# Where the root and the reciprocal of the last RMS norm are taken: one transformer-like block on one core of a Trainium2 chip

## The chip, the cores and the metric

The kernel runs on one core of one Trainium2 chip. The core has a matrix engine (PE, TensorE; its weight loads are shown as PEld), VectorE (DVE), ScalarE (ACT), GpSimd (POOL) and SyncE (SP, which here only issues DMAs), and 16 DMA engines. The metric is the device time of one execution in microseconds (us), median of several runs. All times below are in us unless marked ns.

## What is computed

One block on 512 tokens of width 1024 in fp32: a norm, a mixer of three branches (banded attention, gated spatial mixing, a linear recurrence), a second norm, a mixture of 16 experts of which each token takes two, and a last norm over the sum. The change touches the last norm only:

```
def rms_norm(x, g):
    x32 = x.astype(jnp.float32)
    y = x32 * lax.rsqrt(jnp.mean(x32 * x32, axis=-1, keepdims=True) + EPS)
    return (y * g.astype(jnp.float32)).astype(x.dtype)
...
        x = x + hierarchical_moe(xn, router_grp_w[l], router_grp_b[l], router_exp_w[l], router_exp_b[l],
                                 exp_w_gate[l], exp_w_up[l], exp_w_down[l])
    return rms_norm(x, final_norm_g)
```

## The kernel before

There is no scheduler: each engine's program is written out by hand, in one function for each engine, and semaphores order the engines against each other. From about 480 us to 760 us the experts run. A loop over tiles of 128 token slots takes 16 blocks of expert weights per tile. A block of 128 x 1024 fp32 (512 KB) is loaded by SP into one of two sets of buffers, in pieces of 512 columns (2,048 bytes) for each partition; only the last expert's up-projection comes in pieces of 256 columns (1,024 bytes). The buffers lie in the tiles `raw`, `raw_a`, `raw_c`, `raw_mg`, `macc` and `xn2T`. ACT copies each block, rounded, to `w_hi` (L378), DVE takes the remainder `w_lo` (L389), and PE multiplies with both (L1048 to L1050). `w_hi` and `w_lo` have four slots each, so that ACT waits until PE has released the slot of four blocks ago; SP reuses a buffer when DVE has made its `w_lo`.

Tiles in SBUF are laid out in the order in which they are declared, each at a multiple of 32 bytes in every partition. In the built program `par`, `raw`, `w_hi`, `w_lo`, `ident`, `tile_table` and `stat` come first, then `minus_half` at byte 75,008, `slot_idx`, `att`, and an unused tile named `to_512`. The tiles declared behind it (`probs_third`, `macc`, `x_rows`, `raw_a`, `raw_mg`, `xn2T`, `gf_rows`, `raw_c` and the rest) begin with `probs_third` at byte 75,264, which is 147 x 512. All the large ones among them begin at a multiple of 512 bytes. `xrT`, too, begins at one; DVE reads it 4, 8 and 12 bytes further in at L1624.

At the end, the 512 tokens are handled as NT = 4 tiles t = 0 to 3 of 128 rows and 1024 columns. POOL gathers for each tile the rows of its two experts from HBM (`gather`, L667) into `y_lo(t)` and `y_hi(t)`, both in `raw_mg` but for the last `y_hi`, which is in `raw`. DVE adds the first expert to the residual (`first_sum`, L2060). PE puts the second one and the slots of the last expert tile together in PSUM, and DVE adds them (`last_sum`, L2073); tile 3 takes its second expert by a DVE instruction instead (`second_sum`, L2067). ACT copies the last expert tile's product out of PSUM in two halves before that (`xT_hi`, L1033), and DVE takes the remainders (L2079).

The norm of a tile has then these steps. ACT squares the rows and accumulates the sum in `stat[:, 6, t]` (L1040). DVE multiplies it by 1/1024 and adds EPS (`last_mean`, L2085). POOL raises it to the power -1/2 into `stat[:, 7, t]` (L683). DVE multiplies the rows by that and by the gains `gf_rows` (`last_norm`, L2090), for tile 3 in two halves, and SP stores them (L575, L579). These steps of the four tiles are interleaved in the order of the code at the end of DVE's function.

## Time and profile before

| | |
|---|---|
| median of 3 runs | 780.43 us (780.24 to 780.47) |
| the profiled execution | 782.81 us, of which the span of the trace 780.8 us |
| PE, DVE, ACT, POOL busy | 763.4, 495.2, 449.9, 208.2 us |
| mean granted PE clock in the span | 0.995 of 2.4 GHz |
| moved by DMA | 206.75 MB, 265 GB/s over the span |

The profile is of one execution, recorded by the chip's profiler, which takes a little longer than the others. The span runs from the first instruction to the last. In the timeline a row has its start, its duration, the engine, the line of the kernel, and the operands with their sizes; `x2` or `x3` are like instructions merged into one row. Instructions of one engine overlap a little, so that what one costs its engine is the distance between starts and not its duration.

### The profile page before, as it was taken

The numbers are of one execution on the slowest core, as the hardware profiler recorded it, in microseconds if no ns is written. First come the engines' busy times: TensorE is split into PE (matmuls) and PEld (weight loads), VectorE is DVE, ScalarE is ACT, GpSimd is POOL, SyncE is SP. The second block draws the span as 40 slices with busy tenths as digits, with TensorE's granted clock in tenths as the row PEclk, the third lists the DMA queues.
The fourth block names the chain that finished last, engine by engine and source line by source line (L and its number), as shares of the span: only waits on it lengthen the run. The fifth ranks groups of instructions, "written<-read, shape, count | busy, mean of one in ns | idle before, by whom it ended". The sixth has DMA issues, their size and how long they took to land.

```text
span 780.8 us, 10780 instructions
## 1 busy us (share of the span) xinstructions
PE 763.4 (98%) x3739; PEld 622.4 (80%) x3739; DVE 495.2 (63%) x698; ACT 449.9 (58%) x590; POOL 208.2 (27%) x124
## 2 busy tenths in 40 slices
PE   7999999999999999999999999999999999999994
PEld 4888777777787888888888888888888888888782
DVE  4374476585853302322022468999999998999888
ACT  6244657565653322323222446888888878888862
POOL 3474433232332444344445222000000000000033
PEclk9999999999999999999999999999999999999998
DMA  8489999792222263323336738999999999999965
GB/s 298 136 275 381 371 343 387 263 352 80 57 79 81 82 205 91 109 82 107 92 98 191 272 125 279 407 409 408 409 409 409 409 409 410 408 409 409 401 242 206
DMA packets 134319, 206.75 MB, mean 265 GB/s; under 512 B 10813, under 2 KB 65669, under 8 KB 134278
## 3 DMA queue, kind: packets, MB, share of 16 engines
q1 hardware_dynamic: 129780, 189.94, 66.8%
q0 software_dynamic: 2304, 8.39, 2.9%
q10 hardware_dynamic: 2194, 7.89, 2.5%
q8 instruction: 24, 0.39, 0.2%
q14 instruction: 17, 0.14, 0.0%
HBM read 157.95 MB, written 48.25 MB: 264 GB/s over the span
## 4 chain that ended last, share of the span: by engine, by line
PE 93%; DMA 2%; POOL 1%; DVE 1%; issue 1%; ACT 1%; ACTq 0%; DVEq 0%; SPq 0%; POOLq 0%
PE ps L1048 28%; PE ps L1050 27%; PE ps L1049 27%; PE ps L1336 2%; PE ps L1140 1%; PE ps L1168 1%; PE ps L1151 1%; PE ps L1289 1%; POOL raw_mg L667 1%; PE ps L1263 1%; DMA x<-in_x 1%; PE ps L1343 1%; DMA raw_mg<-slots,slot_idx 1%; PE ps L1065 1%; PE ps L1193 1%
## 5 line engine op out<-in xcount | busy, mean ns | idle before, releaser
L383 POOL TENSOR_TENSOR w_lo<-raw,w_hi 128x1024 fp32r<-128x1024 f32 x72 | 173.2, 2407 | 245.1 <-ACT w_hi L371 245.1
L371 ACT ACTIVATE w_hi<-raw 128x1024 fp32r<-128x1024 f32 x73 | 76.9, 1058 | 183.5 <-PE ps L1050 170.6
L1048 PE MATMUL ps<-xn_hi,w_hi 128*128 128x512 f32 x352 | 140.6, 399 | 0.0
L1050 PE MATMUL ps<-xn_hi,w_lo 128*128 128x512 f32 x352 | 137.2, 390 | 0.0
L1049 PE MATMUL ps<-xn_lo,w_hi 128*128 128x512 f32 x352 | 137.1, 390 | 0.0
L1048 PE MATMUL ps<-w_hi,xT_hi 128*128 128x512 f32 (+1 forms) x248 | 96.7, 390 | 0.0
L1050 PE MATMUL ps<-w_hi,xT_lo 128*128 128x512 f32 (+1 forms) x248 | 95.1, 384 | 0.0
L1049 PE MATMUL ps<-w_lo,xT_hi 128*128 128x512 f32 (+1 forms) x248 | 94.9, 383 | 0.0
L667 POOL DMA_INDIRECT raw_mg<-slots,slot_idx x7 | 7.8, 1113 | 277.4 <-DMA slots<-y_tile 275.6
L1048 PEld LDWEIGHTS ps<-xn_hi,w_hi 128*128 128x128 f32 x352 | 66.1, 188 | 16.2 <-issue 2.5
L1049 PEld LDWEIGHTS ps<-xn_lo,w_hi 128*128 128x128 f32 x352 | 66.1, 188 | 14.1 <-issue 1.0
L1050 PEld LDWEIGHTS ps<-xn_hi,w_lo 128*128 128x128 f32 x352 | 66.1, 188 | 14.0
L1706 DVE SCALAR_TENSOR_TENSOR macc<-raw,ps 128x512 f32<-128x512 f32 x16 | 11.0, 687 | 94.1 <-PE ps L1050 93.8
L389 DVE TENSOR_TENSOR w_lo<-raw_mg,w_hi 128x1024 fp32r<-128x1024 f32 x57 | 67.6, 1219 | 0.6 <-ACT w_hi L378 0.5
L378 ACT ACTIVATE w_hi<-raw_mg 128x1024 fp32r<-128x1024 f32 x57 | 59.0, 1055 | 6.7 <-PE ps L1050 6.5
L389 DVE TENSOR_TENSOR w_lo<-raw,w_hi 128x1024 fp32r<-128x1024 f32 x43 | 51.6, 1219 | 5.0 <-ACT w_hi L378 4.7
L1048 PEld LDWEIGHTS ps<-w_hi,xT_hi 128*128 128x128 f32 x248 | 46.6, 188 | 9.4 <-DVE w_lo L389 0.7
L1050 PEld LDWEIGHTS ps<-w_hi,xT_lo 128*128 128x128 f32 x248 | 46.6, 188 | 9.3
L1049 PEld LDWEIGHTS ps<-w_lo,xT_hi 128*128 128x128 f32 x248 | 46.7, 188 | 8.5
L378 ACT ACTIVATE w_hi<-raw 128x1024 fp32r<-128x1024 f32 x43 | 44.8, 1056 | 14.0 <-PE ps L1050 10.7
L1048 PE MATMUL ps<-w_hi,hT_hi 128*128 128x512 f32 x128 | 51.3, 401 | 0.6 <-DVE hT_lo L1961 0.6
L1050 PE MATMUL ps<-w_hi,hT_lo 128*128 128x512 f32 x128 | 50.0, 390 | 0.0
(311 smaller groups left out, 1477.6 us busy)
## 6 DMA issues: line engine op xcount, KB each, us to landing
slots<-raw SPq DMA_DIRECT2D x65, 512.0 KB, 7.0
raw<-in_w_in SPq DMA_DIRECT2D x52, 512.0 KB, 4.3
raw_mg<-in_exp_w_down SPq DMA_DIRECT2D x35, 512.0 KB, 11.0
raw<-in_exp_w_gate SPq DMA_DIRECT2D x29, 512.0 KB, 11.8
raw_a<-in_exp_w_gate SPq DMA_DIRECT2D x26, 512.0 KB, 10.9
raw_c<-in_exp_w_up SPq DMA_DIRECT2D x24, 512.0 KB, 11.8
raw_mg<-in_exp_w_up SPq DMA_DIRECT2D x22, 512.0 KB, 10.6
raw<-in_exp_w_up SPq DMA_DIRECT2D x15, 512.0 KB, 11.6
```

The lines of the kernel that those rows point to most:

```text
L371: nc.scalar.activation(w_hi[:, b % HI_SLOTS, :], raw_buf(b), ACT.Copy)\
L378: nc.scalar.activation(w_hi[:, (8 + r) % HI_SLOTS, :], buf, ACT.Copy).then_inc(S["hi_act"], 1)
L383: eng.tensor_tensor(w_lo[:, b % HI_SLOTS, :], raw_buf(b), w_hi[:, b % HI_SLOTS, :].bitcast(F32), ALU.subtract)\
L389: nc.vector.tensor_tensor(w_lo[:, (8 + r) % HI_SLOTS, :], place(at, r)[0], w_hi[:, (8 + r) % HI_SLOTS, :].bitcast(F32), ALU.subtract)\
L667: pool.indirect_dma_start(dst, None, slots, bass.IndirectOffsetOnAxis(ap=slot_idx[:, 2 * t + k:2 * t + k + 1], axis=0))\
L1048: pe.matmul(dst, hi_l, hi_r, start=start, stop=False)
L1049: pe.matmul(dst, hi_l, lo_r, start=False, stop=False)
L1050: return pe.matmul(dst, lo_l, hi_r, start=False, stop=stop)
L1065: mm = pe.transpose(ps[:, 2 * t + k // 4, (k % 4) * P:(k % 4 + 1) * P], x0[:, t, k * P:(k + 1) * P], ident[:, :])
L1140: mm = pe.matmul(score_home(g, h)[:, home + k0:home + k1], qT[rows, jp % 2, i * P:(i + 1) * P], kT[rows, jp % 2, k0:k1], start=True, stop= ...
L1336: mm = pe.transpose(ps[:, 3 + k // 4, (k % 4) * P:(k % 4 + 1) * P], rows[:, k * P:(k + 1) * P], ident[:, :])
L1706: dve.scalar_tensor_tensor(out=macc[:, 1, :], in0=gate_buf[:, g % 3, :], scalar=1.0, in1=ps[:, 2 + c, :], op0=ALU.add, op1=ALU.mult)\
```

## The change

ACT takes the root right behind its square of each tile, `sqrt(sum/1024 + EPS)`, with the scale as a constant and EPS from a new tile `eps_col`, and DVE takes the reciprocal of it in place (`last_rstd`), at which `last_norm` multiplies as before. DVE's `last_mean` and POOL's power are gone. DVE waits for ACT (`y_rms`) before its reciprocal, and for its own reciprocal (`y_rstd`) before `last_norm`. ACT waits for its own square (`y_sq`) before the root. Ahead of the last copies, ACT takes the root of `eps_col` once into an unused place, which puts the loading of the root's table there. POOL sets `eps_col` at the start of the kernel.

```diff
--- before.py
+++ after.py
@@ -144,6 +144,7 @@
 
         stat = sb(ctx, "stat", [P, 8, NT])
         minus_half = sb(ctx, "minus_half", [P, 1])
+        eps_col = sb(ctx, "eps_col", [P, 1])
         slot_idx = sb(ctx, "slot_idx", [P, 2 * NT], I32)
         att = sb(ctx, "att", [P, 3, 4])
         sb(ctx, "to_512", [P, 32])
@@ -293,7 +294,7 @@
             "exp_in exp_done scattered tab "
             "x_even_in x_odd_in xT_ps xT_hi_done xT_done silu_done hid_done hT_ps hT_hi_done hT_done "
             "y_act y_even_stored y_odd_stored y_last_stored before_last_stored sel_ps sel_done z_ps "
-            "y_sum y_sq y_stat y_rstd y_norm y_out dve_chain").split()}
+            "y_sum y_sq y_rms y_rstd y_norm y_out dve_chain").split()}
         raw_in = [sem(f"raw_in{s}") for s in range(RAW_MIX)]
         even_in = [sem(f"even_in{s}") for s in range(PER_TILE)]
         odd_in = [sem(f"odd_in{s}") for s in range(PER_TILE)]
@@ -584,6 +585,7 @@
         def _(pool):
 
             pool.memset(ident[:, :], 0.0).then_inc(S["ident_done"], 1)
+            pool.memset(eps_col[:, :], EPS)
             pool.memset(minus_half[:, :], -0.5).then_inc(S["consts_pool"], 1)
             pool.wait_ge(S["ident_done"], 1)
             pool.affine_select(out=ident[:, :], in_=ident[:, :], compare_op=ALU.not_equal, fill=1.0, base=0,
@@ -678,10 +680,6 @@
             for t in range(NT):
                 gather(0, y_lo(t), t)
                 gather(1, y_hi(t), t)
-            for t in range(NT):
-                pool.wait_ge(S["y_stat"], t + 1)
-                pool.tensor_tensor(stat[:, 7, t:t + 1], stat[:, 6, t:t + 1], minus_half[:, :], ALU.pow)\
-                    .then_inc(S["y_rstd"], 1)
 
 
         @block.scalar
@@ -1028,6 +1026,7 @@
                 if s == 10:
                     hT_hi_half(0)
             hT_hi_half(1)
+            act.activation(att[:, 0, 0:1], eps_col[:, :], ACT.Sqrt)
             for c in range(2):
                 act.wait_ge(S["w_used"], loop_block(tiles, 3 + c))
                 act.activation(xT_hi[:, 4 * c:4 * c + 4, :].rearrange("p k n -> p (k n)"), ps[:, 5 + c, :], ACT.Copy)\
@@ -1039,6 +1038,9 @@
                     act.wait_ge(S["y_sq"], t)
                 act.activation(xn2[:, 0, :], y_lo(t), ACT.Square, accum_out=stat[:, 6, t:t + 1])\
                    .then_inc(S["y_sq"], 1)
+                act.wait_ge(S["y_sq"], t + 1)
+                act.activation(stat[:, 7, t:t + 1], stat[:, 6, t:t + 1], ACT.Sqrt, scale=1.0 / D, bias=eps_col[:, :])\
+                   .then_inc(S["y_rms"], 1)
 
 
         @block.tensor
@@ -2080,10 +2082,9 @@
                                   xT_hi[:, 4 * c:4 * c + 4, :].rearrange("p k n -> p (k n)").bitcast(F32),
                                   ALU.subtract).then_inc(S["xT_done"], 1)
 
-            def last_mean(t):
-                dve.wait_ge(S["y_sq"], t + 1)
-                dve.tensor_scalar(stat[:, 6, t:t + 1], stat[:, 6, t:t + 1], 1.0 / D, EPS, ALU.mult, ALU.add)\
-                   .then_inc(S["y_stat"], 1)
+            def last_rstd(t):
+                dve.wait_ge(S["y_rms"], t + 1)
+                dve.reciprocal(stat[:, 7, t:t + 1], stat[:, 7, t:t + 1]).then_inc(S["y_rstd"], 1)
 
             def last_norm(t, at=slice(0, D)):
                 dve.wait_ge(S["y_rstd"], t + 1)
@@ -2100,16 +2101,16 @@
             last_sum(0)
             first_sum(3)
             last_sum(1)
-            last_mean(0)
             second_sum(3)
             last_sum(2)
-            last_mean(1)
+            last_rstd(0)
             last_norm(0)
             last_sum(3)
-            last_mean(2)
+            last_rstd(1)
             last_norm(1)
-            last_mean(3)
+            last_rstd(2)
             last_norm(2)
+            last_rstd(3)
             for c in range(2):
                 last_norm(3, slice(512 * c, 512 * (c + 1)))
```

`eps_col` takes 32 bytes in each partition, between `minus_half` and `slot_idx`. In the built program every tile declared behind it lies 32 bytes further: `probs_third` begins at byte 75,296, and the large tiles behind it begin 32 bytes past a multiple of 512. `raw`, `w_hi`, `w_lo` and `ident` stay where they were.

ACT's program behind the last copy of `hT_hi`, to its end, before (`xn,stat<-raw_mg` is the square with its sum):

```order
L1007 ACTIVATE hT_hi<-ps 128x256
L1032 ISA
L1033 ACTIVATE xT_hi<-ps 128x512
L1032 REGISTER_ALU
L1033 ACTIVATE xT_hi<-ps 128x512
L1040 ACTIVATE xn,stat<-raw_mg 128x1024 x4
```

The same place now:

```order
L1005 ACTIVATE hT_hi<-ps 128x256
L1029 ACT_TABLE_LOAD
L1029 ACTIVATE att<-eps_col 128x1
L1031 ISA
L1032 ACTIVATE xT_hi<-ps 128x512
L1031 REGISTER_ALU
L1032 ACTIVATE xT_hi<-ps 128x512
L1039 ACTIVATE xn,stat<-raw_mg 128x1024
L1042 ACTIVATE stat<-stat,eps_col 128x1
```

A table load and a 128x1 activation stand now ahead of the two copies to `xT_hi`, and a 128x1 activation behind each square; the last two rows repeat three more times. There is no other table load between them.

DVE's program from `last_sum(1)` on, before (L2073 `last_sum`, L2085 `last_mean`, L2067 `second_sum`, L2090 `last_norm`):

```order
L2073 SCALAR_TENSOR_TENSOR raw_mg<-ps,w_first,raw_mg 128x1024
L2085 TENSOR_SCALAR stat<-stat 128x1
L2067 SCALAR_TENSOR_TENSOR raw_mg<-raw,w_first,raw_mg 128x1024
L2073 SCALAR_TENSOR_TENSOR raw_mg<-ps,w_first,raw_mg 128x1024
L2085 TENSOR_SCALAR stat<-stat 128x1
L2090 SCALAR_TENSOR_TENSOR raw_mg<-raw_mg,stat,gf_rows 128x1024
L2073 SCALAR_TENSOR_TENSOR raw_mg<-ps,w_first,raw_mg 128x1024
L2085 TENSOR_SCALAR stat<-stat 128x1
L2090 SCALAR_TENSOR_TENSOR raw_mg<-raw_mg,stat,gf_rows 128x1024
L2085 TENSOR_SCALAR stat<-stat 128x1
L2090 SCALAR_TENSOR_TENSOR raw_mg<-raw_mg,stat,gf_rows 128x1024
L2090 SCALAR_TENSOR_TENSOR raw_mg<-raw_mg,stat,gf_rows 128x512 x2
```

The same now (L2075 `last_sum`, L2069 `second_sum`, L2087 the reciprocal, L2091 `last_norm`):

```order
L2075 SCALAR_TENSOR_TENSOR raw_mg<-ps,w_first,raw_mg 128x1024
L2069 SCALAR_TENSOR_TENSOR raw_mg<-raw,w_first,raw_mg 128x1024
L2075 SCALAR_TENSOR_TENSOR raw_mg<-ps,w_first,raw_mg 128x1024
L2087 RECIPROCAL stat<-stat 128x1
L2091 SCALAR_TENSOR_TENSOR raw_mg<-raw_mg,stat,gf_rows 128x1024
L2075 SCALAR_TENSOR_TENSOR raw_mg<-ps,w_first,raw_mg 128x1024
L2087 RECIPROCAL stat<-stat 128x1
L2091 SCALAR_TENSOR_TENSOR raw_mg<-raw_mg,stat,gf_rows 128x1024
L2087 RECIPROCAL stat<-stat 128x1
L2091 SCALAR_TENSOR_TENSOR raw_mg<-raw_mg,stat,gf_rows 128x1024
L2087 RECIPROCAL stat<-stat 128x1
L2091 SCALAR_TENSOR_TENSOR raw_mg<-raw_mg,stat,gf_rows 128x512 x2
```

Each of the four small instructions moved behind one or two large ones. Before, a mean stood apart from the norm of its tile; now each reciprocal stands directly ahead of the norm that reads it.

## Rows read from the trace of the kernel before

**Rows 1.** The page: busy time, share of the span, instructions; the chain by engine.

```profile
PE 763.4 (98%) x3739; PEld 622.4 (80%) x3739; DVE 495.2 (63%) x698; ACT 449.9 (58%) x590; POOL 208.2 (27%) x124
...
PE 93%; DMA 2%; POOL 1%; DVE 1%; issue 1%; ACT 1%; ACTq 0%; DVEq 0%; SPq 0%; POOLq 0%
```

**Rows 2.** Chain that ended last, from 765 us: start us, us, what.

```profile
760.48 5.62 DMA raw_mg<-slots,slot_idx
...
773.64 1.53 POOL stat L683
...
775.19 1.28 DVE raw_mg L2090
...
777.14 0.66 DVE raw_mg L2090
```

**Rows 3.** Timeline of DVE from 766 us: start us, us, line, operation [idle before].

```profile
766.12 1.28 DVE L2060 SCALAR_TENSOR_TENSOR raw_mg<-raw_mg,w_first,x_rows 128x1024 f32<-128x1024 f32 x1 [0.46 <-DMA raw_mg<-slots,slot_idx]
...
768.52 0.14 DVE L2085 TENSOR_SCALAR stat<-stat 128x1 f32<-128x1 f32 x1
768.58 1.28 DVE L2067 SCALAR_TENSOR_TENSOR raw_mg<-raw,w_first,raw_mg 128x1024 f32<-128x1024 f32 x1
...
773.48 1.27 DVE L2090 SCALAR_TENSOR_TENSOR raw_mg<-raw_mg,stat,gf_rows 128x1024 f32<-128x1024 f32 x1
774.71 0.15 DVE L2085 TENSOR_SCALAR stat<-stat 128x1 f32<-128x1 f32 x1
775.19 2.61 DVE L2090 SCALAR_TENSOR_TENSOR raw_mg<-raw_mg,stat,gf_rows 128x1024 f32<-128x1024 f32 x3 [0.33 <-POOL stat L683]
```

**Rows 4.** Timeline of DVE at 102 us: a reciprocal and what reads it.

```profile
103.12 0.15 DVE L1599 RECIPROCAL att<-att 128x1 f32<-128x1 f32 x1
103.31 0.49 DVE L1601 TENSOR_SCALAR probs<-probs,att 128x512 f32<-128x512 f32 x1
```

**Rows 5.** Timeline of DVE at 35 us: another reciprocal and its reader.

```profile
35.57 0.18 DVE L1527 RECIPROCAL chan<-chan 128x4 f32<-128x4 f32 x1
35.78 0.16 DVE L1528 TENSOR_TENSOR chan<-chan 128x4 f32<-128x4 f32 x1
```

**Rows 6.** Timeline of POOL: the powers of tiles 2 and 3.

```profile
773.64 2.04 POOL L683 TENSOR_TENSOR stat<-stat,minus_half 128x1 f32<-128x1 f32 x2 [0.93 <-DVE stat L2085]
```

**Rows 7.** Timeline of ACT from 757 us.

```profile
757.39 0.38 ACT L1007 ACTIVATE hT_hi<-ps 128x256 fp32r<-128x256 f32 x1 [0.54 <-issue]
760.16 0.60 ACT L1033 ACTIVATE xT_hi<-ps 128x512 fp32r<-128x512 f32 x1 [2.39 <-PE ps L1050]
...
773.53 1.06 ACT L1040 ACTIVATE xn<-raw_mg 128x1024 f32<-128x1024 f32 x1 [1.30 <-DVE raw_mg L2073]
774.50 0.19 ACT L1040 ACTIVATION_READ_ACCUMULATOR xn<-raw_mg 128x1 f32 x1
```

**Rows 8.** Timeline of ACT at 474 us: a table load and a 128x1 activation.

```profile
475.00 1.28 ACT L955 ACT_TABLE_LOAD   x1
476.29 0.20 ACT L955 ACTIVATE att<-minus_half 128x1 f32<-128x1 f32 x1
```

**Rows 9.** DMA queue of the loads, 500 to 700 us: packets, MB, share of 16 engines.

```profile
q1 hardware_dynamic: 37891, 75.98, 97.7%
```

**Rows 10.** The same of 735 to 740 us, when most packets have 1,024 bytes.

```profile
q1 hardware_dynamic: 1864, 1.93, 108.3%
```

**Rows 11.** Timeline of SP: issue of a load into macc at 714 us.

```profile
714.42 0.37 SPq L421 DMA_DIRECT2D macc<-in_exp_w_down  x1
```

**Rows 12.** Tile macc, that load: us from issue to landing.

```profile
DMA to landing us min/median/max: 7.7/7.7/7.7
```

**Rows 13.** Timeline of ACT: the first read of that load.

```profile
727.23 1.05 ACT L378 ACTIVATE w_hi<-macc 128x1024 fp32r<-128x1024 f32 x1
```

**Rows 14.** Source lines: duration ns min/median/max of two 128x512 forms.

```profile
L1624 DVE SCALAR_TENSOR_TENSOR conv<-xrT,par,conv x12: 750/752/753, 70.5 to 178.0; 128x512 f32<-128x512 f32 x12
...
L1556 DVE SCALAR_TENSOR_TENSOR sv_rows<-sv_rows,stat,sgu_g_sb x4: 743/746/746, 60.4 to 62.4; 128x512 f32<-128x512 f32 x4
```

## The prediction

> **What bounds the kernel now.** I read the page first, then the chain that ended last, then the timelines of the last 20 us. PE holds 93% of the chain [rows 1]. Up to about 760 us nothing that a norm's small instructions cost can be seen. The chain then leaves PE: it waits for POOL's gather of tile 3, which lands at 766.10, and from there runs over DVE to the end [rows 2]. DVE stood idle 0.46 before 766.12 and only once more behind it, 0.33 at 775.19 [rows 3]. So the end is 766.12 plus the sum of DVE's starts, plus what follows the last half norm (777.14 to 780.8, the last store and the end of the program). PE, ACT and POOL have gaps there. The 0.33 is a wait for POOL's power of tile 2, which started at 773.64 and took 1.53 [rows 2, 6]. That is the wait which the change is able to remove.
>
> **What goes.** Four means. A mean of 128x1 lasts 0.14, but the next instruction starts 0.06 behind its start (768.52 to 768.58) [rows 3]. For tiles 0 to 2 that makes 3 x 0.06 = 0.18. The fourth mean started at 774.71, 1.23 behind the norm of tile 1, where two large instructions and nothing between them take 2.40, 1.20 each (766.12 to 768.52); so it came 0.03 late, since ACT's square ended at 774.69 [rows 7]. From it to the norm of tile 2 passed 0.48, the 0.33 of waiting included [rows 3]. In all 0.18 + 0.03 + 0.48 = 0.69 of DVE's path goes. POOL's four powers go too. The last of them, of tile 3, lay beside the norm of tile 2 (the 2.04 of [rows 6] from 773.64 hold both, so it ended at 775.68, and its norm started over half a microsecond later). It is worth nothing.
>
> **What comes on DVE.** Four reciprocals, each directly ahead of the norm that reads it, which waits for it. Nothing can cover that wait, since DVE runs in order. A 128x1 reciprocal and its reader stand 0.19 apart, start to start [rows 4]; with four columns it is 0.21 [rows 5]. I take 0.19, the row of the same size: 4 x 0.19 = 0.76. The bounds are 4 x 0.06 = 0.24, if the wait cost no more than a mean does, and 4 x 0.21 = 0.84. What is queued behind the waiting norm is the rest of DVE's program and so the end; nobody else waits for it but SP with the stores.
>
> **What comes on ACT.** A root of 128x1 behind each square. With a like one of 0.20 [rows 8] and some 0.05 for waiting for its own square, tile 3's is done at about 774.50 + 0.19 + 0.25 = 774.94 by the times of before, and at 775.0 when DVE's `last_sum(3)` has moved by 0.07 (two means less, one reciprocal more). Its reciprocal is not due before 776.3, behind the norm of tile 2. The roots of tiles 0 to 2 have more time, since in the new order each reciprocal stands at least one large instruction later than its mean did. So none is waited for. The margin is 1.2, and if a root took 1.5 instead of 0.25 the cost would begin there.
>
> **The table.** The load and the first root stand where ACT was idle for 2.39, from 757.77 to 760.16, waiting for PE [rows 7]. The load takes 1.28 and the next activation starts 1.29 behind it, lasting 0.20 [rows 8]: 1.5, hidden with 0.9 to spare. Without that cover, it would delay the copies to `xT_hi`, and first meet DVE's 0.46 idle. The program has no other load there (the order of ACT in the section on the change), although squares and roots alternate. The Trainium skill (ScalarE: Activation LUTs, What ACT_TABLE_LOAD costs) puts a switch at about 2.66 us, a drain of 1.38 included. By that the first copy would start some 0.5 late, about as much as DVE's wait of 0.46 gives back, and the sum would be the same or a tenth more; the rows show no such drain between an activation and a load.
>
> **What moves.** EPS's memset at the start of POOL is a fraction of a microsecond ahead of the first gathered data: nothing. But `eps_col` also shifts every tile declared behind it by 32 bytes, and with them most landing places of the weights, which stood at multiples of 512 bytes. DVE doesn't mind: reading 4 to 12 bytes past such a multiple takes 752 ns and at one 746 [rows 14]. What it does to a DMA no row of before shows, and the queue is full from 480 us on. Its packets took 97.7% of 16 engines over 200 us, 0.977 x 16 x 200 / 37,891 = 82.5 ns for 2,005 bytes on average [rows 9]. In the stretch of 1,035-byte packets it is 1.083 x 16 x 5 / 1,864 = 46.5 ns [rows 10]. So 970 bytes cost 36.0 ns, and 32 bytes 1.2 ns. From below I bound the shift by nothing. From above, by a further 256 bytes for each packet, 9.5 ns. The value I take is one further 32-byte piece, 1.2 ns, since the pieces of the loads still begin at a multiple of 32 and are shifted by just one. With 37,891 / 16 x 242 / 200 = 2,866 packets for an engine from 480 to 722 us, that makes the loads 3.4 late at 722. They can be: a load into `macc` issued at 714.42 landed 7.7 later, at 722.1, and ACT first read it at 727.23 [rows 11 to 13]. The reserve there is 5.1. It would shrink to 1.7, and PE would see nothing.
>
> The Trainium skill (DMA: Bandwidth & Descriptors, How a descriptor splits into AXI transactions) has transactions start at multiples of 256 bytes and charges whole 32-byte beats. By it I estimate 65 beats for 2,048 bytes begun 32 past such a multiple, in place of 64, 1.6% more, about 3.7 us over the stretch: inside the reserve also.
>
> **The sum.** 780.8 - 0.69 + 0.76 = 780.87 for the span, 782.88 for the profiled execution in place of 782.81, which is +0.07. The profiled one lies 2.38 above the median of the runs, and I take the same distance: 780.43 + 0.07 = 780.5. With the bounds of the wait it is 780.0 to 780.6. With some tenths for the gathers and stores of shifted rows, the likeliest case has 780.0 to 781.2.
>
> **Rivals.** (a) *The shift slows the loads*, slower. The point from which it decides is 5.1 us / 2,866 = 1.8 ns for a packet. Two 32-byte pieces, one at each end, would be 2.4 ns, 6.8 us, 1.7 beyond the reserve: 782.2. The upper bound of 9.5 ns makes 27.2, 22.1 beyond it: 802.6. For it speaks that the DMA engines are full and that the reserve is no more than 5.1; against it, that all places keep the multiple of 32, and that only more than one and a half pieces count. (b) *The roots are late*, or each change between square and root costs a table load after all. Then a tile takes ACT 1.14 + 0.25 + 2 x 1.3 = 4.0 against the 2.45 at which DVE supplies the tiles, and four of them from 765.70 end at 781.9, which would give about 786. Against it is the order of ACT, with one load. (c) *It does what it says and gains*: waits without price on DVE, -0.69 + 0.24 = -0.45: 780.0. This lies inside the likeliest case, and no row offers more: even with all four reciprocals free it would be 779.7.
>
> **How the numbers follow.** A measurement here tells about 0.2% from no change, 1.6 us. Likeliest case with (c): 0.83, all within 0.2%. (a): 0.13, slower. (b): 0.01, slower. Unforeseen: 0.02 faster, 0.01 slower. So 0.02 faster, 0.83 same, 0.15 slower. The range of 8 in 10 is 779.9 to 782.3: the likeliest case and the near end of (a).
>
> **What would show it.** In the profile of the changed kernel: no DVE wait behind 766.1, 0.19 from each reciprocal to its norm, no POOL behind the gathers, the last half norm at about 777.2, one table load near 757.8 that ends before 759.2, and a root of 0.2 to 0.3. Of (a): packets at over 83.7 ns from 500 to 700 us, a reserve of `macc`'s load at 714 us that falls below 5.1 by 1.2 for each 0.4 ns, and, if it decides, ACT waiting for a DMA before its reads of `raw_a`, `raw_c` or `macc`, with PE idle after it. The prediction is wrong if the queue slows by more than 2.2%, or if something that the trace of before can't show waits for the root.

## The result, and the profile after

The changed kernel took 797.82 us (median of 5 runs, 796.86 to 800.26), the kernel before, beside it, 780.47 (5 runs, 780.24 to 781.70). The ratio is 1.0224, with a 95% interval of 1.0213 to 1.0235. The change makes the kernel 17.4 us slower; 780.5 had been predicted, with 782.3 as the end of the range. The profiled execution took 800.26, of which the span of the trace is 798.5. The mean granted clock of PE is 0.995, as before.

The page after, for [rows 1]:

```profile
PE 779.8 (98%) x3739; PEld 622.9 (78%) x3739; DVE 492.0 (62%) x698; ACT 453.3 (57%) x596; POOL 203.8 (26%) x121
...
PE 93%; DMA 2%; DVE 1%; issue 1%; POOL 1%; ACT 0%; POOLq 0%; ACTq 0%; DVEq 0%; SPq 0%
```

PE is busy 16.4 longer (763.4 before) with the same 3,739 instructions. So nothing new runs on PE, and what runs there takes longer. DVE, ACT and POOL moved by 3 to 4 us, down, up and down.

Where it is longer: two stretches of either kernel, one in the mixer, where the DMA engines are half idle, and one among the experts, where they are full. The view shows, by stretch: us, busy time (and number of instructions) of PE, PEld, DVE, ACT and POOL, the granted clock, the share of 16 DMA engines, GB/s. Before:

```profile
60.00:440.00 380.00, 380.00 (x1887) 307.56 (x1886) 160.28 (x258) 165.52 (x258) 151.00 (x74) 1.00 0.55 187
500.00:700.00 200.00, 199.99 (x947) 165.86 (x946) 188.07 (x204) 166.82 (x181) 0.00 (x0) 1.00 1.05 409
```

After:

```profile
60.00:440.00 380.00, 380.00 (x1837) 299.92 (x1836) 150.06 (x246) 162.39 (x251) 148.61 (x74) 1.00 0.52 178
500.00:700.00 200.00, 200.00 (x929) 162.93 (x928) 185.02 (x200) 163.62 (x176) 0.00 (x0) 1.00 1.05 398
```

PE is busy without a gap in all four and its clock is granted in full (1.00, the level of 2.4 GHz). But in the same 380 us it ran 1,887 matmuls before and 1,837 after, 2.7% fewer, and in the 200 us of the experts 947 and 929. DVE and ACT do less as well, in step with PE, which they feed. This holds in the mixer too, where the DMA share is 0.52, so it is no matter of loads that come late.

The groups of PE's instructions, kept apart by shape (count, then busy time and mean ns of one, then idle time ahead). Before:

```profile
L1049 PE MATMUL ps<-xn_lo,w_hi 128*128 128x512 f32 x352 | 137.1, 390 | 0.0
...
L1049 PE MATMUL ps<-w_lo,xT_hi 128*128 128x512 f32 x232 | 90.4, 390 | 0.0
```

After:

```profile
L1051 PE MATMUL ps<-xn_lo,w_hi 128*128 128x512 f32 x352 | 139.0, 395 | 0.0
...
L1051 PE MATMUL ps<-w_lo,xT_hi 128*128 128x512 f32 x232 | 91.7, 395 | 0.0
```

Each matmul is recorded 5 ns longer. The recorded length covers an overlap with the next one, so the distance of starts is the better measure. The timeline of PE around 300 us, before and then after; the two kernels are at different matmuls there (`xn` and `br` are streamed), but the shape is the same. Before:

```profile
299.68 0.39 PE L1049 MATMUL ps<-xn_lo,w_hi 128*128 128x512 f32 x1
299.90 0.39 PE L1050 MATMUL ps<-xn_hi,w_lo 128*128 128x512 f32 x1
300.13 0.39 PE L1048 MATMUL ps<-xn_hi,w_hi 128*128 128x512 f32 x1
300.36 0.39 PE L1049 MATMUL ps<-xn_lo,w_hi 128*128 128x512 f32 x1
300.58 0.39 PE L1050 MATMUL ps<-xn_hi,w_lo 128*128 128x512 f32 x1
```

After:

```profile
299.80 0.39 PE L1051 MATMUL ps<-br_lo,w_hi 128*128 128x512 f32 x1
300.03 0.40 PE L1052 MATMUL ps<-br_hi,w_lo 128*128 128x512 f32 x1
300.27 0.39 PE L1050 MATMUL ps<-br_hi,w_hi 128*128 128x512 f32 x1
300.50 0.40 PE L1051 MATMUL ps<-br_lo,w_hi 128*128 128x512 f32 x1
300.74 0.39 PE L1052 MATMUL ps<-br_hi,w_lo 128*128 128x512 f32 x1
```

Four distances make 0.90 before and 0.94 after. Over all matmuls of 128x512 that read `w_hi` or `w_lo`, the mean distance (those under 260 ns, so without waits) is 227.4 ns before and 233.3 after where `w` is the second name of a row, and 227.7 and 233.1 where it is the first one. The longest unbroken run of them has 798, in the mixer: 797 distances in 180.68 us before (254.10 to 434.77) and in 185.97 after (257.80 to 443.77), 226.70 and 233.34 ns each. At 2.4 GHz these are 544 and 560 cycles, 16 more. The kernel has 1,344 of the former kind and 1,512 of the latter: 1,344 x 5.9 + 1,512 x 5.4 = 16.1 us. That agrees with 15.6, by which the stretch from the first such matmul to the last with `hT` grew (746.4 to 762.0; kernels laid out alike agree in this stretch within 0.4). Of the two names in a matmul's row, the first is what is streamed through the array in 512 columns, and the second is what was loaded as weights: 3 x 448 matmuls of the mixer have `w` as weights, while the other 3 x 504, the experts' among them, stream it.

Another 3.1 us lie behind the last expert. The two make 18.7 where the spans differ by 17.7 (780.8 and 798.5), because in the profile of before the first such matmul starts 1.1 later (14.7 us into the span, 13.6 after). The chain that ended last, for [rows 2], and DVE's timeline, for [rows 3]:

```profile
777.45 6.33 DMA raw_mg<-slots,slot_idx
```

```profile
781.26 1.28 DVE L2062 SCALAR_TENSOR_TENSOR raw_mg<-raw_mg,w_first,x_rows 128x1024 f32<-128x1024 f32 x1 [2.58 <-DMA raw_mg<-slots,slot_idx]
...
783.80 1.29 DVE L2062 SCALAR_TENSOR_TENSOR raw_mg<-raw_mg,w_first,x_rows 128x1024 f32<-128x1024 f32 x1
...
788.59 0.15 DVE L2087 RECIPROCAL stat<-stat 128x1 f32<-128x1 f32 x1
788.78 1.28 DVE L2091 SCALAR_TENSOR_TENSOR raw_mg<-raw_mg,stat,gf_rows 128x1024 f32<-128x1024 f32 x1
...
793.96 0.15 DVE L2087 RECIPROCAL stat<-stat 128x1 f32<-128x1 f32 x1
794.15 1.42 DVE L2091 SCALAR_TENSOR_TENSOR raw_mg<-raw_mg,stat,gf_rows 128x512 f32<-128x512 f32 x2
```

DVE waited 2.58 for the gathers, where it had waited 0.46. POOL gathers when the last store of `y_tile` to `slots` has landed. From issue to landing it took, before and then after:

```profile
DMA to landing us min/median/max: 2.6/2.6/2.6
```

```profile
DMA to landing us min/median/max: 4.4/4.4/4.4
```

That is 1.8 more, and from the first gather to the landing of tile 3's passed 15.7 (768.13 to 783.78) in place of 14.3. The two add up to 3.2. The store was late while loads were still under way: before, the last load of weights had landed at 748.06 and the store was issued at 748.33; after, it was issued at 762.83 and the last load landed at 766.04.

The loads' queue from 500 to 700 us, for [rows 9]:

```profile
q1 hardware_dynamic: 37052, 74.19, 97.9%
```

By the same working as in the prediction a packet takes 0.979 x 16 x 200 / 37,052 = 84.6 ns, 2.1 more than before. Among the records of single packets of 2,048 bytes, nine in ten took 84 ns before; now the mean is 86.4, more than half still take 84, and the slowest tenth takes 93 or more.

Which packets are the longer ones can be told by their loads. A packet's record doesn't name its tile, but a load of 512 KB has 256 such packets, and where loads landed one right behind the other, 250 to 262 of them ended between two landings. I gave these to the second landing, which blurs the borders between loads, and took the median over the loads of a tile. For 11 such loads into `raw`, which didn't move, a packet takes 84.0 ns. For 23 into `raw_a`, `raw_c` and `raw_mg`, which did, it takes 87.9 to 88.1, and nearly eight in ten packets are longer. So the packets that land in a shifted tile take 4 ns more on average in such stretches. The 2.1 of the whole queue is less, since some quarter of the loads goes to `raw`, and since beside other transfers, of 4,096-byte packets, fewer of the shifted packets are longer.

The load into `macc` that [rows 11 to 13] show (issue, landing, first read):

```profile
728.32 0.37 SPq L422 DMA_DIRECT2D macc<-in_exp_w_down  x1
```

```profile
DMA to landing us min/median/max: 10.0/10.0/10.0
```

```profile
741.39 1.05 ACT L379 ACTIVATE w_hi<-macc 128x1024 fp32r<-128x1024 f32 x1
```

It landed 10.0 behind its issue at 728.32, at 738.3, and was read at 741.39. The reserve shrank from 5.1 to 3.1 and didn't run out: no engine waited for a load of weights here.

ACT's timeline around the table load and at the last root, for [rows 7, 8]:

```profile
771.88 0.38 ACT L1005 ACTIVATE hT_hi<-ps 128x256 fp32r<-128x256 f32 x1 [0.55 <-PE ps L1407]
772.28 1.28 ACT L1029 ACT_TABLE_LOAD   x1
773.57 0.20 ACT L1029 ACTIVATE att<-eps_col 128x1 f32<-128x1 f32 x1
774.69 0.60 ACT L1032 ACTIVATE xT_hi<-ps 128x512 fp32r<-128x512 f32 x1 [0.91 <-PE ps L1052]
...
792.26 0.19 ACT L1039 ACTIVATION_READ_ACCUMULATOR xn<-raw_mg 128x1 f32 x1
792.47 0.29 ACT L1042 ACTIVATE stat<-stat,eps_col 128x1 f32<-128x1 f32 x1
```

The table load and the first root lie in ACT's idle time, with 0.91 to spare. The last root is done at 792.76. Its reciprocal starts at 793.96.

### The profile page after: what moved, and what is told of

It reads as the page before. It is cut to its first block, busy times and chain, and to the rows that moved or that the text cites. A ratio compares the mean times of both kernels' runs of the same rounds, so it can differ in the third digit from the quotient of the medians.

```text
span 798.5 us, 10783 instructions
## 1 busy us (share of the span) xinstructions
PE 779.8 (98%) x3739; PEld 622.9 (78%) x3739; DVE 492.0 (62%) x698; ACT 453.3 (57%) x596; POOL 203.8 (26%) x121
## 4 chain that ended last, share of the span: by engine, by line
PE 93%; DMA 2%; DVE 1%; issue 1%; POOL 1%; ACT 0%; POOLq 0%; ACTq 0%; DVEq 0%; SPq 0%
PE ps L1050 28%; PE ps L1051 27%; PE ps L1052 27%; PE ps L1338 2%; PE ps L1142 1%; PE ps L1170 1%; PE ps L1153 1%; PE ps L1291 1%; PE ps L1265 1%; DMA raw_mg<-slots,slot_idx 1%; PE ps L1345 1%; POOL raw_mg L669 1%; DMA x<-in_x 1%; PE ps L1067 1%; DMA slots<-y_tile 1%
## 5 line engine op out<-in xcount | busy, mean ns | idle before, releaser
L1050 PE MATMUL ps<-xn_hi,w_hi 128*128 128x512 f32 x352 | 142.4, 405 | 0.0
L1051 PE MATMUL ps<-xn_lo,w_hi 128*128 128x512 f32 x352 | 139.0, 395 | 0.0
L1052 PE MATMUL ps<-xn_hi,w_lo 128*128 128x512 f32 x352 | 139.0, 395 | 0.0
L1052 PEld LDWEIGHTS ps<-xn_hi,w_lo 128*128 128x128 f32 x352 | 66.0, 187 | 16.1
L1052 PEld LDWEIGHTS ps<-w_hi,xT_lo 128*128 128x128 f32 x248 | 46.6, 188 | 10.5
L1051 PE MATMUL ps<-w_lo,hT_hi 128*128 128x512 f32 x128 | 50.6, 395 | 0.0
```

The source lines that it names most:

```text
L1050: pe.matmul(dst, hi_l, hi_r, start=start, stop=False)
L1051: pe.matmul(dst, hi_l, lo_r, start=False, stop=False)
L1052: return pe.matmul(dst, lo_l, hi_r, start=False, stop=stop)
```

## The experiments

The theory after the result: the new tile `eps_col` moved nearly all tiles by 32 bytes, and this alone costs 17 us; most of it because PE's two operands no longer lie alike. Rivals were that the new instructions cost it, and that the DMA engines, writing to shifted places, do. Times are medians, the distances are means over the two kinds of matmul told above, and "PE" is the stretch from the first matmul with `w` to the last with `hT` (start to start), "rest" that from there to the end of the span. The rows from e6 to e9 and e11 are of one run each, and the runs of the kernel before went from 779.7 to 782.3, so their times are good to about 1 us; their distances and packets are means over many hundreds of records. "Packet" is worked out from the row of the queue from 500 to 700 us, as above.

| kernel | us | kernel before beside it | `w` as weights, ns | `w` streamed, ns | packet, ns | PE, us | rest, us |
|---|---|---|---|---|---|---|---|
| before | 780.47 | | 227.4 | 227.7 | 82.5 | 746.4 | 19.7 |
| after | 797.82 | 780.47 | 233.3 | 233.1 | 84.6 | 762.0 | 22.8 |
| e1_shift_only | 798.73 | 780.97 | 233.3 | 233.1 | 84.5 | 761.1 | 22.8 |
| e2_repadded | 780.73 | 780.97 | 227.4 | 227.6 | 82.3 | 746.2 | 19.5 |
| e3_w_slots_32 | 796.54 | 780.97 | 233.3 | 233.3 | 82.2 | 761.2 | 19.6 |
| e4_dma_dest_32 | 788.00 | 780.97 | 227.4 | 227.7 | 84.6 | 748.6 | 25.0 |
| e5_both_32 | 792.04 | 781.66 | 227.4 | 227.8 | 85.6 | 752.5 | 24.6 |
| e6_w_slots_64 | 791.48 | 781.66 | 233.3 | 229.4 | 82.3 | 756.4 | 20.1 |
| e6_w_slots_128 | 796.32 | 781.66 | 233.0 | 232.6 | 82.2 | 760.4 | 19.6 |
| e7_dma_dest_128 | 786.67 | 781.66 | 227.4 | 227.6 | 84.6 | 747.0 | 24.8 |
| e8_dest_256_part | 781.38 | 780.87 | 227.4 | 227.6 | 82.4 | 746.2 | 19.8 |
| e9_w_slots_16 | 792.61 | 780.87 | 231.9 | 231.7 | 82.3 | 757.2 | 19.6 |
| e9_w_slots_96 | 798.44 | 780.87 | 234.2 | 233.4 | 82.3 | 763.2 | 19.4 |
| e10_early_rstd | 780.63 | 780.87 | 227.4 | 227.8 | 82.3 | 746.4 | 19.2 |
| e11_distance_256 | 780.43 | 780.71 | 227.4 | 227.8 | 82.3 | 746.0 | 19.6 |

The granted clock is 0.994 to 0.996 in all of them.

**The shift without the change.** The kernel before with one unused tile:

```diff
         minus_half = sb(ctx, "minus_half", [P, 1])
+        sb(ctx, "eps_col", [P, 1])
         slot_idx = sb(ctx, "slot_idx", [P, 2 * NT], I32)
```

> The kernel before with one unused tile of 32 bytes declared between minus_half and slot_idx, and nothing else: every tile declared behind it begins 32 bytes later, none of the norm's instructions changes. If the shift of the addresses makes the loss, it takes 797 to 799 us and PE's large matmuls stand 231 to 235 ns apart from 20 us on, as in the changed kernel. If the moved instructions of the last norm make it, it stays at 780.5 us with 227 ns.

It took 798.73, a ratio of 1.0228 (1.0208 to 1.0249). Apart from addresses, not one instruction is different from the kernel before, and the whole loss is there: the longer distances, the longer packets and the longer rest. Its stretch in the mixer, with the 1,837 instructions of the changed kernel:

```profile
60.00:440.00 380.00, 380.00 (x1837) 299.94 (x1836) 149.11 (x243) 161.65 (x249) 147.52 (x71) 1.00 0.52 177
```

**The change without the shift.** The changed kernel, in which the unused tile `to_512` gives back the 32 bytes:

```diff
-        sb(ctx, "to_512", [P, 32])
+        sb(ctx, "to_512", [P, 24])
```

> The changed kernel with the unused tile to_512 cut from 128 to 96 bytes, so that all tiles behind it begin where they did before: the whole change without the shift. If the shift makes the loss: 780.5 us (780.0 to 780.6 by the sum over DVE), ratio to before 0.9995 to 1.0005, large matmuls 227 ns apart. If the instructions make it: 797 us.

It took 780.73 (10 runs) against 780.97 (13 runs), a ratio of 0.9998 (0.9988 to 1.0007). So the instructions cost nothing that can be told, and the loss is that of the layout. DVE's timeline at its end:

```profile
764.53 1.29 DVE L2062 SCALAR_TENSOR_TENSOR raw_mg<-raw_mg,w_first,x_rows 128x1024 f32<-128x1024 f32 x1 [0.34 <-DMA raw_mg<-slots,slot_idx]
...
774.69 0.15 DVE L2087 RECIPROCAL stat<-stat 128x1 f32<-128x1 f32 x1
774.88 1.42 DVE L2091 SCALAR_TENSOR_TENSOR raw_mg<-raw_mg,stat,gf_rows 128x512 f32<-128x512 f32 x2
```

The norm of the last half starts 0.67 behind that of the half before it, whose row holds both: at 775.55, 11.02 behind `first_sum(3)`. Before, it started at 777.05 by its own record ([rows 3] have it within the last row), 10.93 behind 766.12. So the new form is 0.08 longer. Its last reciprocal and the norm stand 0.19 apart.

**Only `w_hi` and `w_lo` shifted.** This leaves every landing place of a DMA where it was, and moves one of PE's two operands (and `ident` with the five small tiles behind it, which no large matmul reads):

```diff
         raw = sb(ctx, "raw", [P, 6, 1024])
+        sb(ctx, "pad_w", [P, 8])
         w_hi = sb(ctx, "w_hi", [P, HI_SLOTS, 1024], F32R)
...
-        sb(ctx, "to_512", [P, 32])
+        sb(ctx, "to_512", [P, 24])
```

> The kernel before with w_hi, w_lo, ident and tile_table begun 32 bytes later (to_512 shorter by as much): all places of DMAs and all other operands keep their multiples of 512. Theory A, PE reads an operand more slowly when it begins 32 bytes past a multiple of 512 (or 64): w_hi and w_lo are the streamed operand in the expert stage and the weights in the mixer stage, so PE's matmuls go from 227 to 231 to 235 ns in both and the time to 790 to 800 us. Theory B, misplaced DMA writes take from PE's bandwidth or from the DMA queue: nothing changes, 780.5 us.

It took 796.54, a ratio of 1.0200 (1.0180 to 1.0221). Its two stretches in the same view as above:

```profile
60.00:440.00 380.00, 380.00 (x1837) 300.40 (x1836) 148.89 (x243) 161.78 (x249) 147.04 (x71) 1.00 0.52 177
500.00:700.00 200.00, 200.00 (x928) 162.49 (x927) 184.40 (x200) 164.13 (x177) 0.00 (x0) 1.00 1.05 409
```

PE ran 1,837 and 928 instructions, where the changed kernel ran 1,837 and 929, but the DMA engines moved the 409 GB/s of the kernel before. So the longer distance needs no slower DMA. PE's stretch grew by 14.8, the rest not at all. This kernel loses 15.6 us, and the changed one 17.4.

**Only the landing places shifted.** `raw` was moved behind `ident` and set off by 32 bytes, and `raw_a`, `raw_c` and `raw_mg` got 32 bytes ahead of them, with as much less in the paddings behind. `macc` and `xn2T`, which also take weights, stay at multiples of 512, unlike in the changed kernel; `raw`, which stayed there, is shifted here:

```diff
-        raw = sb(ctx, "raw", [P, 6, 1024])
         w_hi = sb(ctx, "w_hi", [P, HI_SLOTS, 1024], F32R)
...
         ident = sb(ctx, "ident", [P, P])
+        sb(ctx, "pad_r", [P, 8])
+        raw = sb(ctx, "raw", [P, 6, 1024])
...
+            sb(s2, "pad_ra", [P, 8])
             raw_a = sb(s2, "raw_a", [P, 3, 1024])
...
+            sb(s2, "pad_rc", [P, 8])
             raw_c = sb(s2, "raw_c", [P, 4, 1024])
...
-            sb(s3, "pad_a3", [P, AREA_A])
+            sb(s3, "pad_a3", [P, AREA_A + 8])
             raw_mg = sb(s3, "raw_mg", [P, 8, 1024])
```

> The kernel before with the landing places of the weights, raw, raw_a, raw_c and raw_mg, begun 32 bytes past a multiple of 512, and every operand of the large matmuls kept at one. Theory A: PE stays at 227 ns and the time at 780.5 us. Theory B: the loss of the changed kernel, 790 to 798 us, and PE's matmuls at 231 to 235 ns or PE waiting. The packets of 2,048 bytes take 84 ns before and on average 86.4 ns after; by their landing places they go up here too in either theory.

It took 788.00, a ratio of 1.0091 (1.0071 to 1.0111): 7 us. The matmuls' distance is that of before. The queue from 500 to 700 us:

```profile
q1 hardware_dynamic: 36799, 73.57, 97.3%
```

The packet takes 0.973 x 16 x 200 / 36,799 = 84.6 ns, as in the changed kernel. Here the reserve does run out. The waits from 480 to 780 us (in total, times, longest), and the landing of the last `y_tile` store:

```profile
DVE raw_mg L2063 <- DMA raw_mg<-slots,slot_idx: 5.6, 3, 2.6
ACT w_hi L381 <- DMA raw_mg<-in_exp_w_down: 5.6, 6, 1.8
```

```profile
DMA to landing us min/median/max: 6.2/6.2/6.2
```

PE's stretch grew by 2.2; 5.3 lie behind it, where the store took 3.6 more and the gathers came 1.6 more apart. The store was issued at 749.14, and the last load of weights landed at 755.81. In e3, where the packets are as before, it was issued at 761.55, 0.57 behind the landing of the last load, and took 2.6.

E4's 7.0 and e3's 15.6 make 22.6, more than the 17.8 of e1. The difference has a place: in e1 PE's stretch grew by 14.7, by no more than in e3, and the rest by 3.1 in place of 5.3. So 14.8 + 0 + 3.1 = 17.9. That fits a PE that takes 2.5% longer and so also asks for the weights 2.5% later: the last load landed 3.5 behind the issue of the last store in e1 (761.19 and 764.72), against 6.7 in e4. The two kernels don't shift the same landing places, though, so how much of it is due to PE's pace was not measured by itself.

**Everything shifted alike.** The same 32 bytes one tile earlier, ahead of `raw`, so that `w_hi` and `w_lo` move as well:

```diff
         w_first = sb(ctx, "w_first", [P, 2, NT])
+        sb(ctx, "pad_r", [P, 8])
         raw = sb(ctx, "raw", [P, 6, 1024])
```

> The kernel before with 32 unused bytes ahead of raw: raw, w_hi, w_lo, ident and everything behind them begin 32 bytes past a multiple of 512, so that the streamed operand, the weights and the DMA places are shifted alike. If each operand that begins off its multiple costs 16 cycles (6.7 ns) of a matmul, both together make 240 ns and some 812 us. If a matmul pays once whichever is off, 233 ns and 797 to 799 us. If only the distance between the two operands counts, PE is back at 227 ns and what remains is the loss of the shifted DMA places, 787 to 789 us.

It took 792.04, a ratio of 1.0136 (1.0104 to 1.0168), less than e1, although more was shifted. PE's groups (idle time ahead and what ended it at the end of a row):

```profile
L1049 PE MATMUL ps<-w_hi,xT_hi 128*128 128x512 f32 x232 | 92.7, 400 | 3.4 <-DVE xT_lo L1955 3.4
...
L1050 PE MATMUL ps<-xn_lo,w_hi 128*128 128x512 f32 x352 | 137.1, 390 | 0.0
...
L1050 PE MATMUL ps<-w_lo,xT_hi 128*128 128x512 f32 x232 | 90.5, 390 | 0.0
```

The matmuls are back at 390 ns, where the changed kernel has 395, and their distance at 227.4 and 227.8. So it is not the place of the operands that costs PE but their distance from each other. What is left is the DMA's side: the row of the queue (36,301 packets, 97.1%) makes 85.6 ns for a packet, a further 1.0. PE's stretch grew by 6.1, with 3.4 of waiting at these matmuls. Part of the further 1.0 is that here `macc` and `xn2T` are shifted too. Counted by loads as above, the packets of 2,048 bytes into `xn2T` take 84.0 in e4 and 88.1 here, and those into `raw`, `raw_a`, `raw_c` and `raw_mg` 88.0 in both. The two tiles take 15 of the 132 loads from 500 to 700 us, which is worth 15 / 132 x 4 = 0.5 by this estimate. The rest stays open; what also differs is that here the tile into which the experts' rows are loaded (`xn2`) and the sources of all stores are shifted.

**Other distances.** As e3 with 64, 128, 96 and, by a common tile for both, 16 bytes (`pad_w` of 16, 32 and 24 columns, `to_512` smaller by as much); and as the kernel before with `to_512` of 96 columns, by which all behind it is shifted by 256 bytes and `w` is not.

> As e3_w_slots_32, with w_hi, w_lo, ident and tile_table 64 bytes past a multiple of 512 in place of 32. If PE fetches in lines of 64 bytes, nothing is off any more: 227 ns, 780.5 us. If the line is longer, 233 ns (or more, if the cost goes with the bytes) and 795 us or above.

> The same with 128 bytes. If the line is 64 or 128 bytes: 227 ns and 780.5 us. If only multiples of 256 or 512 are free of cost: 233 ns and 795 us.

> As e3_w_slots_32, with w_hi and w_lo 16 bytes past a multiple of 512 (half of the smallest step at which tiles are laid out). If what counts is whether both operands begin in the same piece of 32 or 64 bytes, 16 bytes cost nothing: 227 ns, 780.5 to 781.7 us. If each byte of distance counts, 229 to 233 ns and 788 to 797 us. If a small distance spreads the reads better than none, below 227 ns and below 780 us.

> As e3_w_slots_32 with 96 bytes. The matmuls stand 227 ns apart at a distance of 0 between the two operands (also when both lie 32 off), 233 at 32 either way, 229 or 233 at 64 and 232.5 to 233 at 128. If 0 is the one good distance, 229 to 233 ns and 790 to 797 us. If the cost goes down again with some distance, below 229 ns and below 790 us.

> The kernel before with to_512 256 bytes longer, so that w_hi and w_lo stay at multiples of 512 and everything behind att begins 256 bytes past one: the two operands of each large matmul are 256 bytes apart, and the landing places begin at a multiple of 256, which cost the packets nothing in e8_dest_256_part. If the distance counts modulo 256: 227 ns and 780.5 to 781.7 us. If it counts modulo 512: 229 to 234 ns and 788 to 797 us. If a distance of half of 512 keeps the two reads out of each other's way better than none, below 227 ns and below 780 us.

With 64 bytes it took 791.48, with 128 796.32, with 16 792.61, with 96 798.44, each in one run: 1.2% to 2.2% above the kernel before. All but one of their distances lie between 231.7 and 234.2 ns; the one is 64 bytes with `w` streamed, 229.4. By the counts above that is 1,344 x 5.9 + 1,512 x 1.7 = 10.5 us for 64 bytes, and PE's stretch grew by 10.0. With 256 bytes it is 780.43 against 780.71, one run each, with the distances of before. So a distance of 256 bytes is as good as none, and each of the others tried (16, 32, 64, 96 and 128) costs 4 to 16 cycles for each matmul on average. That the distance counts by its remainder modulo 256 is the simplest rule that fits; distances of 160 bytes or more other than 256 were not tried. No distance tried is faster than zero. The dependence on the distance is not simple: 64 is cheaper than 32 and 96, and it matters there which of the operands is streamed.

**Other landing places.** As e4 with 128 bytes, and, for `raw_a`, `raw_c` and `raw_mg` alone, with 256:

```diff
+            sb(s2, "pad_ra", [P, 64])
             raw_a = sb(s2, "raw_a", [P, 3, 1024])
...
+            sb(s2, "pad_rc", [P, 64])
             raw_c = sb(s2, "raw_c", [P, 4, 1024])
...
-            sb(s3, "pad_a3", [P, AREA_A])
+            sb(s3, "pad_a3", [P, AREA_A + 64])
```

> As e4_dma_dest_32, with the landing places of the weights 128 bytes past a multiple of 512 in place of 32. If a packet pays for every boundary of 256 bytes that it begins off, in whole pieces of 32 bytes, 128 bytes are as bad as 32 or worse (4 further pieces, 4.8 ns, 88.8 ns for 2,048 bytes: over 790 us). If only multiples of 64 or 128 count, the packets are back at 84.0 ns and the time at 780.5 us.

> The kernel before with raw_a, raw_c and raw_mg (not raw, macc and xn2T) 256 bytes past a multiple of 512; the operands of the large matmuls stay. With 32 and with 128 bytes about half of the 2,048-byte packets took longer than 84 ns (mean 86.5 and 86.7). If the landing place must begin at a multiple of 512, some third of the packets is longer here too and the time 782 to 787 us. If a multiple of 256 is enough, nearly all take 84 ns and the time is 780.5 to 781.7 us. PE's large matmuls stay at 227 ns either way.

The queue's row with 128 bytes (36,952 packets, 97.7%) makes 84.6 ns, and with 256 it makes 82.4:

```profile
q1 hardware_dynamic: 37958, 75.97, 97.7%
```

So 128 bytes cost about what 32 do (786.67 us), and 256 nothing (781.38 against 780.87, whose own runs go up to 781.65). Counted by loads as above, a packet that lands 128 bytes off takes 88.6 ns on average in e7, one that lands 32 off 88.0, and one that lands 256 off 84.0 (e8). The Trainium skill (DMA: Bandwidth & Descriptors, How a descriptor splits into AXI transactions) has transactions begin at multiples of 256 bytes. It says so of reads; the boundary agrees with these rows, in which only the place of the write moved. Its count of 32-byte beats fits less well: it would give one beat more for 32 bytes and four more for 128. At 1.2 ns for 32 bytes, the prediction's value, that is an estimate of 1.2 and 4.8 ns; the packets that land shifted take 4.0 and 4.6 more.

**The reciprocals earlier.** In the kernel of e2, the reciprocals of tiles 0 to 2 stand one large instruction ahead of their norm, so that their wait is covered:

```diff
             second_sum(3)
-            last_sum(2)
             last_rstd(0)
+            last_sum(2)
+            last_rstd(1)
             last_norm(0)
             last_sum(3)
-            last_rstd(1)
-            last_norm(1)
             last_rstd(2)
+            last_norm(1)
             last_norm(2)
```

> The changed kernel without the shift (as e2_repadded), with the reciprocals of tiles 0, 1 and 2 moved one large instruction ahead of the norm that reads them, which covers the wait. Each then costs its queue 0.06 us in place of 0.19, so that from DVE's first_sum(3) to its last half norm pass 11.0 - 3 x 0.13 = 10.6 us, against 10.9 in the kernel before. The time goes to some 780.1 us, 0.05% less than before, which these rounds can hardly tell from no change.

DVE's timeline:

```profile
764.73 1.28 DVE L2062 SCALAR_TENSOR_TENSOR raw_mg<-raw_mg,w_first,x_rows 128x1024 f32<-128x1024 f32 x1 [0.42 <-DMA raw_mg<-slots,slot_idx]
...
768.32 0.16 DVE L2087 RECIPROCAL stat<-stat 128x1 f32<-128x1 f32 x1
768.39 1.26 DVE L2075 SCALAR_TENSOR_TENSOR raw_mg<-ps,w_first,raw_mg 128x1024 f32<-128x1024 f32 x1
...
774.47 0.16 DVE L2087 RECIPROCAL stat<-stat 128x1 f32<-128x1 f32 x1
774.67 1.41 DVE L2091 SCALAR_TENSOR_TENSOR raw_mg<-raw_mg,stat,gf_rows 128x512 f32<-128x512 f32 x2
```

The next large instruction starts 0.07 behind a reciprocal that nobody waits for (0.19 in e2), and from `first_sum(3)` to the norm of the last half it is 10.60 in place of 11.02. The 0.4 is there in the trace, and not in the time: 780.63 (10 runs) against 780.87 (13), a ratio of 0.9996 (0.9986 to 1.0006).

None of the kernels is measurably faster than the one before. The 0.4 lies within the spread of the runs (779.65 to 781.48), which can neither show nor exclude it.

## Why the prediction was wrong

**What bounds the kernel.** Right that PE does, and that is why the loss is so large. The reading stopped at the end of the program, though, since only there did the *instructions* change. PE's 93% of the chain was taken as a fixed amount.

**The sum of the last norm.** Right, step by step. Predicted was +0.07 on DVE. In e2, the change with the layout of before, the same stretch takes 0.08 longer by single records. The reciprocals cost 0.19 each before their norm, DVE waits for nothing but its own reciprocals between the gathers and the end, and POOL's powers are gone. In the changed kernel the norm of the last half starts at 794.82, 11.02 behind `first_sum(3)` as in e2. The roots took 0.29 and not 0.20, and their margin was 1.2 as told: done at 792.76, due at 793.96. The one table load began 0.02 behind the last copy of `hT_hi`, and the first root ended 0.9 before the next copy, as told. Rival (b) fell. (Its own sum is off by 0.2: four tiles of 4.0 from 765.70 end at 781.7.) Rival (c) didn't happen, since the wait does have its price, 0.19.

**What moves: the step that failed.** The prediction saw that `eps_col` shifts every tile behind it by 32 bytes, and that `w_hi` and `w_lo` stay. It then asked who reads or writes the shifted tiles, and named DVE and the DMA queue. PE was not asked. Its term was nothing, without a row or a reason for it. PE reads its streamed operand and its weights from two tiles, and `xn`, `br`, `xT` and `hT` had moved against `w_hi` and `w_lo`. In place of nothing that term is 14.8 to 15.6 us (e3, and the stretch of the changed kernel), 5.4 to 5.9 ns for each of 2,856 matmuls. No row of before gave a price for it, and so, by the rule the prediction set itself for the DMA, it would have needed a bound. Even 1% on PE, 7 us, would have put the far end of the range beyond 787 and the mechanism among the rivals. The chance of 0.83 for "the same" rested on a list of readers that wasn't complete.

**The DMA's term** was mis-sized. Taken were 1.2 ns for every packet; measured are 2.1 on average (2.4 among those of 2,048 bytes), made up of up to 4 ns for those that land shifted and nothing for the others. The average is near the case of rival (a), "two 32-byte pieces" at 2.4, and beyond its point of 1.8; that it comes so close is luck, since the piece it counts in is not what a shifted packet pays. By its formula 2.1 x 2,866 = 6.0 less 5.1 gives 0.9 late on PE. With the landing places alone shifted PE's stretch grew by 2.2 (e4, 32 bytes) and 0.6 (e7, 128 bytes). In e5, with 3.1 ns more for a packet, the formula gives 3.8 and the stretch grew by 6.1. So its direction holds, and its size only roughly. Two things were missing from it. The rest behind PE: a full queue of longer packets also delays the last store of `y_tile` (2.6 to 6.2 in e4, to 4.4 in the changed kernel) and the gathers behind it, 5.3 and 3.1 us, on the path that sets the end. "Some tenths for the gathers and stores" was the estimate. And in the changed kernel PE was slower itself; the reserve only fell to 3.1, and rival (a)'s wait for a load never came. The direction of rival (a) came true, by another mechanism.

**The estimate from the Trainium skill** for the queue (DMA: Bandwidth & Descriptors, How a descriptor splits into AXI transactions), 1.6% or 3.7 us, was as low as the value taken (3.4): measured are 2.1 / 82.5 = 2.5%, 6.0 us.

**The signs named in advance.** Packets at over 83.7 ns was met with 84.6, and a queue slower by more than 2.2% with 2.5%. Both pointed at the DMA, which made the smaller part of the loss. No sign named PE's matmuls, and nothing waited for the root.

## What to carry to other kernels

A new tile is an edit of the layout as well: list every tile that it moves and every engine that reads them, PE's two operands first, and pad so that nothing moves by anything but a multiple of 256 bytes. Where PE bounds a kernel, a change that adds no instruction for it can still lengthen each of its matmuls; compare the distance of their starts in a stage that the change doesn't touch. An unused tile that only pads, as `to_512` here, is a sign to look for such a dependence.

## What the runs showed of the hardware

**Matmul.** A matmul of 128x512 in fp32r, behind which the next weights of 128x128 are loaded while it streams (the load is recorded with 188 ns and starts within 0.01 of the matmul), stands 544 cycles from the next at 2.4 GHz (226.70 ns in the run of 798, before and in e5 alike) when the streamed tile and the weights' tile begin at the same remainder modulo 256 bytes: with both at 0 (before, e4), both at 32 (e5) and 256 apart (e11) it is the same. At the other distances tried it is more: 560 with 32, and by the means told above 4 to 16 more with 16, 64, 96 and 128. That two reads of one partition get in each other's way when they differ so is my reading of it; no run here shows the reads themselves.

**DMA.** In stretches of loads alone, a packet of 2,048 bytes from HBM took 84.0 ns when it landed at a multiple of 256 bytes (before, e8), 88.0 on average 32 bytes past one (e4, e5, the changed kernel) and 88.6 at 128 (e7). Nearly eight in ten of the shifted packets are longer at 32 and nearly nine in ten at 128; the others take 84 still. Over the whole queue, with the packets that landed in place and those of other transfers, that made 84.6 ns in place of 82.5.

**Small instructions.** A 128x1 activation with its bias from a tile took 0.29, one with constants 0.20. A table load started 0.02 behind an activation's end, took 1.28, and the next activation started 0.01 behind it. A reciprocal of 128x1 costs DVE 0.19 with a reader that waits for it and 0.07 without.
